# Keeping the last expert block's rows on chip: a one-core trunk layer with a mixture of experts

## The reference, cut to what matters

```python
def trunk_layer(x, ...):                                   # T = 1024 prompt + 64 sample tokens, D = 1024
    z = rms_norm(x, norm1_g) @ w_in                        # 12 chunks of 128 columns: pool, value, gate
    ...pooling mixer, conv mixer...
    x = x + concat([y_pool, y_conv]) @ w_out + b_out
    hm = rms_norm(x, norm2_g)
    x = x + hier_moe(hm, ...)                              # then the final rms_norm with norm_f_g

def hier_moe(h, ...):
    ...group g_sel, top 2 of its 8 experts: eid[token, 2], gates[token, 2]
    order = argsort(flat_e)                                # rows sorted by expert, blocks of 128 rows
    yb = (silu(xb @ w_eg[e]) * (xb @ w_eu[e])) @ w_ed[e]   # per block
    y = zeros.at[buf_tok].add(yb * buf_gate[:, None])      # each token adds its two rows
```

## Time and profile before

| what | us |
|---|---|
| median of 3 runs (991.07 to 991.28) | 991.25 |
| the profiled execution's own time | 992.78 |
| its span, first to last instruction | 990.9 |
| TensorE busy (share of the span) | 945.9 (95%) |
| VectorE busy | 840.9 (85%) |
| ScalarE busy | 586.6 (59%) |
| GpSimd busy | 168.4 (17%) |
| mean granted TensorE clock | 0.988 |

### The profile page before, as it was taken

The page is one execution under the profiler, slowest core; times in us unless marked ns, Lnnn a source line. Parts: engine busy times, 40 slices in busy tenths (PEclk is TensorE's granted clock), DMA queues, the critical chain, the costliest instruction groups (busy, mean ns, idle before and its releaser), DMA issues.

```text
span 990.9 us, 14018 instructions
## 1 busy us (share of the span) xinstructions
PE 945.9 (95%) x4771; PEld 801.5 (81%) x4771; DVE 840.9 (85%) x978; ACT 586.6 (59%) x564; POOL 168.4 (17%) x201
## 2 busy tenths in 40 slices
PE   5999999999999989999999999999999999999973
PEld 5999978987888777788888888888888888888751
DVE  6488998988687697999898998989989899898857
ACT  7311111574532144888777887778877788777514
POOL 1000000000000021632231222312223122231210
PEclk9999999999999979999999999999999999999997
DMA  9321251314332846899999999999999999999988
GB/s 286 118 65 43 67 154 58 112 34 161 128 128 86 329 130 222 335 403 378 401 370 389 378 379 392 384 385 391 387 403 379 397 392 380 397 389 384 340 267 311
DMA packets 68028, 275.72 MB, mean 278 GB/s; under 512 B 12783, under 2 KB 27631, under 8 KB 43417
## 3 DMA queue, kind: packets, MB, share of 16 engines
q1 hardware_dynamic: 56281, 255.97, 68.7%
q0 software_dynamic: 9792, 17.85, 4.7%
q10 hardware_dynamic: 1920, 1.44, 0.6%
HBM read 259.34 MB, written 31.38 MB: 293 GB/s over the span
## 4 chain that ended last, share of the span: by engine, by line
PE 57%; DVE 4%; DMA 2%; ACT 1%; issue 1%; SPq 0%; POOLq 0%; POOL 0%; DVEq 0%; ACTq 0%
PE ps L1234 11%; PE ps L1236 11%; PE ps L1235 11%; PE ps L1253 6%; PE ps L1251 6%; PE ps L1252 6%; PE ps L1206 3%; DVE big L1808 2%; PE ps L1260 1%; DMA y_scratch<-arena,cur 1%; ACT arena L947 1%; DMA arena<-y_scratch 1%; DVE arena L1905 0%; PE ps L1347 0%; PE ps L1190 0%
## 5 line engine op out<-in xcount | busy, mean ns | idle before, releaser
L1808 DVE TENSOR_TENSOR big<-arena,big 128x2048 fp32r<-128x2048 f32 x128 | 286.9, 2283 | 0.0
L843 ACT ACTIVATE big<-arena 128x2048 fp32r<-128x2048 f32 x128 | 238.8, 1910 | 3.5 <-DMA arena<-in_w_eg 1.8
L1234 PE MATMUL ps<-big,ring 128*128 128x512 f32 x508 | 201.1, 396 | 3.2 <-DVE big L1808 3.2
L1236 PE MATMUL ps<-big,ring 128*128 128x512 f32 x508 | 198.0, 390 | 0.0
L1235 PE MATMUL ps<-big,ring 128*128 128x512 f32 x508 | 197.6, 389 | 0.0
L1808 DVE TENSOR_TENSOR slot_tail<-arena,slot_tail 128x2048 fp32r<-128x2048 f32 x62 | 138.9, 2281 | 0.0
L843 ACT ACTIVATE slot_tail<-arena 128x2048 fp32r<-128x2048 f32 x62 | 115.5, 1918 | 0.2 <-DVE eob L1784 0.2
L1234 PEld LDWEIGHTS ps<-big,ring 128*128 128x128 f32 x508 | 95.4, 188 | 22.6 <-DVE big L1808 4.0
L1236 PEld LDWEIGHTS ps<-big,ring 128*128 128x128 f32 x508 | 95.3, 188 | 20.3
L1235 PEld LDWEIGHTS ps<-big,ring 128*128 128x128 f32 x508 | 95.5, 188 | 18.7
L1251 PE MATMUL ps<-slot_tail,hTr 128*128 128x512 f32 x248 | 99.2, 400 | 0.0
(11 more groups left out here) (280 smaller groups left out, 1485.3 us busy)
## 6 DMA issues: line engine op xcount, KB each, us to landing
arena<-in_w_eg SPq DMA_DIRECT2D x64, 1024.0 KB, 8.5
arena<-in_w_eu SPq DMA_DIRECT2D x64, 1024.0 KB, 9.5
arena<-in_w_ed SPq DMA_DIRECT2D x64, 1024.0 KB, 9.9
arena<-in_x_prompt SPq DMA_DIRECT2D x16, 512.0 KB, 5.1
arena<-y_scratch SPq DMA_DIRECT2D x16, 512.0 KB, 8.8
arena<-in_w_in SPq DMA_DIRECT2D x12, 512.0 KB, 4.0
arena<-in_conv_band SPq DMA_DIRECT2D x8, 576.0 KB, 4.3
arena<-in_w_out SPq DMA_DIRECT2D x8, 512.0 KB, 4.1
```

Of the source, the lines that this page charges most:

```text
L843: act.activation(we_h[n % SLOTS], raw[n % RAWS], ACT.Copy).then_inc(high_done, 1)
L1234: pe.matmul(out, part_h[b][:, k, :], wh[:, i, :], start=(k == 0), stop=False)
L1236: ins = pe.matmul(out, part_l[b][:, k, :], wh[:, i, :], start=False, stop=(k == KD - 1))
L1808: dve.tensor_tensor(we_l[n % SLOTS], raw[n % RAWS], we_h[n % SLOTS].bitcast(F32), ALU.subtract).then_inc(low_done, 1)
```

## The change

1. Block 31's rows are no longer scattered. ScalarE copies the product out of PSUM times a per-row gate (`own_h`), VectorE makes the low part (`own_l`, in `keep_low`). A 0/1 matrix per tile (`at_token`), built by VectorE from the slot table, puts row i on its token when TensorE multiplies it by `own_h` and `own_l`. The gate of each row comes by way of DRAM: ScalarE writes the gates (`gate_dram`), POOL gathers one per row (`gate_row`). For this `set_gates` runs before the low parts of the last two pieces.
2. The second rows of all tokens are set to zero early (`zero_second`), because those of block 31 are now never written. SP waits only for the scatter of block 30 before it loads second rows, each tile has its own semaphore and place, and no load waits for a sum.
3. TensorE sums gate times second row and block 31's row for all 9 tiles, and the residual too for tiles 1 and 2; VectorE adds the residual for the other 7 (`add_late`). The 40 idle transposes ahead of the sums are gone.
4. Head: weight chunks are stored so that a chunk is contiguous; (0, 0) is made tile by tile in matmuls of 128, 128 and 108 columns behind tiles 2, 3 and 4, the idle transposes of tiles 2 and 3 are gone, and (1, 0) and (0, 1) follow in pieces.
5. First pair: the two empty scatters move ahead of the wait for `hm_out`; VectorE makes the first rows' low part before `overflow_counts`, pieces 7 and 9 before `hidden` and `overflow_plan`.

```diff
@@ over_loop @@
+        def over_loop(eng, body, ahead=None):      # runs ahead() only if there is an overflow pair
...
@@ sync @@
-                src = w_in[0, :, CHUNKS[j]:CHUNKS[j] + P].rearrange("(k p) n -> p k n", p=P)
-                sp.dma_start(w_raw[j % 3].rearrange("p (k n) -> p k n", k=KD), src).then_inc(w_in_s[j % 3], 16)
+                sp.dma_start(w_raw[j % 3], w_in_chunk[CHUNKS[j] // P, :, :]).then_inc(w_in_s[j % 3], 16)
...
+            def zero_second(t):
+                r = ROWS[t]
+                dst = y2_dram[2 * t * P:2 * (t * P + r), :].rearrange("(p k) n -> p k n", k=2)[:, 1, :]
+                src = MS.rearrange("p t e -> p (t e)")[0:r, 0:D // 4].unsqueeze(1).to_broadcast([r, 4, D // 4])
+                sp.dma_start(dst.rearrange("p (a n) -> p a n", a=4), src).then_inc(zeroed, 16)
+            sp.wait_ge(const_done, 1)
             for j in (4, 5, 6, 7, 8, 9):
                 load_w_in(j)
+                for t in range(j - 4, NT, 6):
+                    zero_second(t)
...
             for b in range(2):
                 sp.wait_ge(gath[b], 16 * n_pairs + 16)
-                sp.wait_ge(scat[b], 16 * n_pairs + 16)
-            for t in range(FB):
+            sp.wait_ge(scat[0], 16 * n_pairs + 16)
+            sp.wait_ge(f_half, 1)
+            for t in range(NT):
+                if t >= FB:                                  # FB was 6, is 4
+                    sp.wait_ge(f_half, t - FB + 1)
                 load_second(t)
...
-                if t + FB < NT:
-                    if t in ON_PE:
-                        sp.wait_ge(f_sum_pe, sums_of(t)[1])
-                    else:
-                        sp.wait_ge(f_acc, sums_of(t)[0])
-                    load_second(t + FB)
@@ scalar @@
+            act.wait_ge(gates_set, 1)
+            act.dma_start(gate_dram.rearrange("(t p) o -> p (t o)", p=P), gates[:, 1, :],
+                          allow_slow_non_contiguous=True).then_inc(gates_out, 16)
             result(PAIRS - 1, 0)
             hidden_high(PAIRS - 1, 1)
-            result(PAIRS - 1, 1, end=True)
-            over_loop(act, over_body)
+            act.wait_ge(piece_used, after(PAIRS, EARLIER[-1], True))
+            act.wait_ge(gate_in, 16)
+            act.activation(own_h, ye_ps, ACT.Copy, scale=gate_row).then_inc(own_high, 1)
...
+            for t in range(NT):
+                if t == 4:
+                    act.wait_ge(f_in[0], 16)
+                act.activation(gate_diag[t], ident[:, :], ACT.Copy, scale=gates[:, 1, t:t + 1]).then_inc(diag_set, 1)
@@ tensor @@
+            BY_TILE = {2: (0, P), 3: (P, 2 * P), 4: (2 * P, IW)}
-            PIECEWISE = {4: ((0, 0, 3),), 5: ((0, 3, 6),), 6: ((0, 6, 8),), 7: ((1, 0, 3),), 8: ((1, 3, 8),)}
+            PIECEWISE = {5: ((1, 0, 0, 3),), 6: ((1, 0, 3, 6),), 7: ((1, 0, 6, 8), (0, 1, 0, 3)), 8: ((0, 1, 3, 8),)}
...
-            quiet_ps = banks(7, 1)
-            for i in range(40):
-                pe.transpose(quiet_ps[:, i % 4 * P:(i % 4 + 1) * P], ident[:, :], ident[:, :])
...
+            pe.wait_ge(own_high, 1)
+            pe.wait_ge(own_low, 1)
+            for t in range(NT):
+                r = ROWS[t]
+                pe.wait_ge(f_half, t + 1)
+                if t in ALL_ON_PE:                           # (1, 2)
+                    for c0 in (0, BANK):
+                        pe.matmul(f_sums[t][0:r, c0:c0 + BANK], ident[0:r, 0:r], x_in[t][0:r, c0:c0 + BANK], start=True, stop=False)
+                elif t - 4 in ALL_ON_PE:
+                    pe.wait_ge(f_y, t - 3)
+                elif t >= 4:
+                    pe.wait_ge(f_acc, added(t - 4))
+                pe.wait_ge(diag_set, t + 1)
+                pe.wait_ge(f_in[t], 16)
+                for c0 in (0, BANK):
+                    out = f_sums[t][0:r, c0:c0 + BANK]
+                    pe.matmul(out, gate_diag[t][0:r, 0:r], y_second[t][0:r, c0:c0 + BANK], start=t not in ALL_ON_PE, stop=False)
+                    pe.matmul(out, at_token[t][:, 0:r], own_h[:, c0:c0 + BANK], start=False, stop=False)
+                    ins = pe.matmul(out, at_token[t][:, 0:r], own_l[:, c0:c0 + BANK], start=False, stop=True)
+                ins.then_inc(f_late, 1)
@@ vector, body(0, first=True) @@
-                    overflow_counts()
                 rows_low(j, 0)
                 if first:
+                    overflow_counts()
                     overflow_blocks()
                     rows_low(j, 1)
...
                 low(j, 6)
-                if not first:
+                if first:
+                    low(j, 7)
+                else:
                     rows_low(j, 1)
                 hidden(j, 0)
-                low(j, 7)
+                if not first:
+                    low(j, 7)
                 low(j, 8)
+                low(j, 9)
                 if first:
                     overflow_plan()
-                low(j, 9)
                 hidden_low(j, 0)
                 low(j, 10)
                 low(j, 11)
@@ vector, end @@
+            dve.memset(gate_row, 0.0)
+            set_gates()
+            dve.engine_nop().then_inc(gates_set, 1)
             ...low parts of LAST, hidden(PAIRS - 1, 1)...
-            set_gates()
+            ...tok_row, tok_in, and two is_equal that write at_token...
+            def keep_low():
+                dve.wait_ge(own_high, 1)
+                dve.scalar_tensor_tensor(own_l, ye_ps, gate_row, own_h.bitcast(F32), ALU.mult, ALU.subtract).then_inc(own_low, 1)
+            def add_late(t):
+                r = ROWS[t]
+                dve.wait_ge(f_half, t + 1)
+                dve.wait_ge(f_late, t + 1)
+                dve.tensor_tensor(x_in[t][0:r, :], f_sums[t][0:r, :], x_in[t][0:r, :], ALU.add).then_inc(f_acc, 1)
+            for t in range(6):
+                add_first(t)
+            keep_low()
+            for t in range(6, NT):
+                add_first(t)
+            dve.wait_ge(gf_in, 16)
             for t in range(NT):
-                add_first(t)
-            for t in range(NT):
-                if t not in ON_PE:
-                    combine(t)
+                if t not in ALL_ON_PE:
+                    add_late(t)
                 ...final(t - 1)...
@@ gpsimd @@
+            pool.wait_ge(gb_in, 32)
+            for b in range(2):
+                scatter(b, s_idx[:, 0:1])
             ...waits for hm_out, x2_out, x2tr_done...
-            for b in range(2):
-                scatter(b, s_idx[:, 0:1])
             pool.wait_ge(idx_done, 1)
             gather(0, g_idx)
...
+            pool.wait_ge(gates_out, 16)
+            pool.indirect_dma_start(out=gate_row, out_offset=None, in_=gate_dram,
+                                    in_offset=bass.IndirectOffsetOnAxis(ap=g_idx[:, E - 1:E], axis=0),
+                                    bounds_check=last_token, oob_is_err=False).then_inc(gate_in, 16)
             pool.sem_inc(cur_done, 1)
             store_rows(PAIRS - 1, 0)
-            pool.sem_inc(cur_done, 1)
-            store_rows(PAIRS - 1, 1)
```

More of the change, by code:

```diff
@@ L200, in trunk_kernel @@
         gf_bc = arena[:, 2 * NT * D:(2 * NT + 1) * D]
[L201 removed]
+        y_second = [arena[:, (2 * NT + 1 + s) * D:(2 * NT + 2 + s) * D] for s in range(FB)] + y_first[0:NT - FB]
+        assert (2 * NT + 1 + FB) * D <= SZ_V + SZ_U + SZ_H + SZ_W + SZ_S1 + SZ_T + SZ_S2 + SZ_X
+        own_h, own_l = big[:, 4 * HP:4 * HP + D], big[:, 4 * HP + D:4 * HP + 2 * D]
+        at_token = [big[:, 8 * HP + t * P:8 * HP + (t + 1) * P] for t in range(KD)] + [hot_mem[:, 0:P]]
+        assert 8 * HP + KD * P <= 2 * KD * T and SLOTS >= 4
         assert RAWS * HP == 12 * D
[L205 removed]
+        ALL_ON_PE = (1, 2)
         ident = sb("ident", [P, P])
@@ L228, in trunk_kernel @@
         act_t = plin.rearrange("p g d -> p (g d)")
-        gate_diag = [plin[:, i, :] for i in range(len(ON_PE))]
+        gate_diag = [plin[:, t, :] for t in range(4)] + [r_g[:, t * P:(t + 1) * P] for t in range(NT - 4)]
         stat = sb("stat", [P, 6, NT])
@@ L284, in trunk_kernel @@
         ye_ps = banks(5, 2)
-        f_sums = {t: banks(2 * i, 2) for i, t in enumerate(ON_PE)}
+        f_sums = [banks(t % 4 * 2, 2) for t in range(NT)]
         const_done = sem("const_done")
@@ L290, in trunk_kernel @@
         xt_in = [sem("xt_in0"), sem("xt_in1")]
-        xa_in = [sem(f"xa_in{t}") for t in range(NT)]
+        tile_in = [sem(f"tile_in{t}") for t in range(NT)]
         wo_in = [sem(f"wo_in{s}") for s in range(4)]
@@ L320, in trunk_kernel @@
             "zero_done"))
-        f_x = [sem(f"f_x{t}") for t in range(NT)]
-        f_in = [sem(f"f_in{s}") for s in range(FB)]
+        f_in = [sem(f"f_in{t}") for t in range(NT)]
         f_half = sem("f_half")
@@ L325, in trunk_kernel, with added @@
         f_out = sem("f_out")
[L326 to L331, removed]
+        diag_set, f_late = sem("diag_set"), sem("f_late")
+        own_high, own_low, gates_set = map(sem, ("own_high", "own_low", "gates_set"))
```

(23 more changed lines are left out.)

104 lines of the change are left out of this document (57 added, 47 removed).

## The result

The changed kernel takes 1004.14 us at the median of four executions (1002.82 to 1006.66), the kernel before 991.26 beside it: a ratio of 1.0125, 95% interval 1.0105 to 1.0145. The forecast was 988.8 (985.0 to 995.5). The profiled execution took 1002.82 (span 1001.0), 10.0 more than the profiled one of before, where the steps had it 2.5 less: a miss of 12.5 us.

What follows compares the result with a forecast made beforehand. TensorE was taken to bound the loop, without slack; head -2.5, first pair -2.7 and end +2.7 sum to -2.5 us, so 991.25 becomes 988.8 us, range 985.0 to 995.5 (own range 986.3 to 991.3).

Steps and rivals of the forecast that it cites:

- Head: Start of the kernel: narrow products at 0.11 us each let (0, 2) start at 37.7, not 40.22: -2.5 us.
- rival (b): Head: narrow products cost two passes, +5.1 us, total 996.4; chance 0.13.
- First pair: First pair of blocks: earlier gather and low parts, two stalls gone: -2.7 us, bounds -3.75 to 0.
- POOL now finds its two empty scatters done ... 0.8 earlier: First pair: with the empty scatters moved ahead, the gather goes out near 360.8, 0.8 us earlier, bounds 0.6 and 1.0.
- What comes late next: First pair: the 4.0 us plan now stands ahead of pieces 10 and 11, leaving 2.7 of the 3.75 us gain.
- Rival (d): First pair gains nothing, its gather and loads landing when they did: total +0.2, 991.5 us; chance 0.10.
- the gates' trip: End: gates' store takes 7.3 us, gather 1.3; block 30 leaves 1.4 us later, under the backlog: no cost.
- Rival (a): End: gates' store takes 14.6 us and delays block 30's scatter; total +2.1, 993.4 us; chance 0.17.
- the start without the trip: End: TensorE's first sum at 956.7, 17.9 us after block 30's copy, when second rows land.
- the load of the first second rows: End: after block 30's scatter lands at 949.7, first second rows land at 956.5, between 954.5 and 960.9.
- the sums: End: 29.3 us from TensorE's start to tile 8's add, VectorE slower from tile 3; 19.5 us before.

Runs made afterwards that it cites:

- run 7: Kernel before with the new head alone (chunked weights, narrow first products): 989.33 us, ratio 0.9977 to the kernel before.
- run 3: Kernel before with the new head and the new order of the first pair, old end kept: 988.86 us, ratio 0.9969.
- run 4: Changed kernel with the gates stored as 128 runs of 36 bytes, not 1152 elements of 4 bytes (block 31's gates wrong): 996.17 us, ratio 1.0037.
- run 2: Changed kernel with gates made and stored during the first pair instead of behind the last: 998.72 us, ratio 1.0071.
- run 5: Changed kernel without the gates' store and gather: VectorE applies each token's gate, own part of tiles 0 to 3 made early: 989.44 us, ratio 0.9978.
- run 6: run 5's kernel with first rows of tiles 6 to 8 loaded behind second rows of tiles 1 to 3: 987.82 us, ratio 0.9956.
- run 9: The kernel of run 6 measured again, unchanged, in five rounds beside the kernel before: 987.36 us, ratio 0.9951.

## Why the prediction was wrong

*Head: right in mechanism, and near in size.* (0, 2) was forecast at 37.7 and starts at 37.32, with 0.11 us a product; rival (b), two passes, falls. By the router 0.5 us more had come, which I had not forecast. Alone the head is worth 2.3 us of the median (run 7).

*First pair: half wrong.* No stall is left before pieces 7 and 9, as forecast. The step "POOL now finds its two empty scatters done ... 0.8 earlier" failed: the gather goes out at the same time with or without them (358.30 in run 7, 358.25 in run 3). In run 7 the second empty scatter ends 0.5 us after the index is written; in run 3 nothing stands ahead, and GpSimd still takes 0.83 us from the end of that write to the gather, where I had counted 0.30. What comes late next was priced at 1.0 and is 1.6 in those two traces. Rival (d), -0 instead of -2.7, was nearer: 0.7 in the traces of runs 7 and 3, 1.2 in the changed kernel's, both within the spread of single profiles.

*End: the step that failed is the gates' trip.* The prediction said "The nearest row is the router's load, 1024 pieces of 144 B, 7.3 us" and "Nothing, at that price". The store of 1152 pieces of 4 bytes took 21.8, and its price went to two waits at once. Rival (a) named this mechanism and its price was too small too: 14.6 us, 993.4. The router's load was the wrong row: when its pieces moved, only SyncE's own queue moved (975 packets under 512 B from 23.6 to 25.0 us), so its 7.3 us hold almost nothing of what pieces cost beside another queue; the gates' pieces moved beside rows that took 94.1%. In the same place 144 packets did land in 7.2 us (run 4), and the trip then held block 30's scatter up by 1.1 us, the gather. What the strided store costs with the queue empty no run shows. The Trainium skill (DMA: Bandwidth & Descriptors, Rules for kernel authors) says that a strided last dimension becomes one descriptor per element; the trace agrees, 1168 packets, and that rule should have outweighed a row of 144-byte pieces.

*End: the start without the trip.* I put it at 17.9 us after block 30's copy, "nearer the fast end because block 31's scatter no longer moves in that stretch". It is 21.2 to 23.2 (runs 2, 4, 5), at the slow end of my bounds or beyond. Block 30's scatter took the 8.8 us that I had priced (8.0 to 8.8 in these runs). The term that was too small is the load of the first second rows: 6.8 us from issue to landing (949.7 to 956.5), and 10.8, 9.3 and 12.0 in the runs. It stands behind the first rows of tiles 6 to 8, and with those out of its way it took 7.2 and 8.4 (runs 6 and 9). Run 4, which keeps the trip, starts 3.6 us later than forecast: 1.1 is the gather, 2.5 this load.

*End: the sums.* 30.5 against 29.3, but by another bound: TensorE, not VectorE (the stretches above; run 5, with less on TensorE, has 23.6). The low clock was there as forecast, 0.50 (1.2 GHz) from 963 to 966 after 19 us of waiting, but the first tile took 5.1 us where I had 4.1. From tile 3 on TensorE takes 2.64 us a tile, where I had VectorE at 2.76; that the whole is so near is in part luck.

Taken together 7.2 us of the miss are pieces, 3.6 the gather and the load of second rows, 1.2 sums, 0.6 the two front parts. With nothing but the 7.2 put into the forecast, its end is +9.9 and its sum +4.7: a loss. And with the pieces gone the change still loses: run 4 is 4.2 us above the kernel before.

## What to carry to other kernels

Price a DMA by its number of pieces and by what fills the engines at that moment, and take the row for it from a stretch with the same load; and ask who waits behind the engine that waits. Before a transfer is taken off the end by adding work, look at what stands ahead of it in the queue: here three loads in another order came out level with the same order and a block kept on chip. Values that an engine already holds by token need no trip by row: move the multiplication to where the factor is.

## What the runs showed that I had not expected

One store of 4.5 KB took 7.2, 21.8, 23.7 and 37.3 us, by its pieces and by the loads beside it. It also held those loads up: they moved at 162 GB/s beside 1168 packets and at 414 beside 144, and in the last case a gather that TensorE needed came 5.19 us late. The scatter of block 31 took 3.3 or 7.8 us by the order of three loads. The first gather of rows, in two profiles of one kernel, let TensorE start its first turn at 368.19 (run 6) or 366.58 (run 9), and block 30's copy came at 937.81 or 933.67; what sets that spread was not settled, and it is larger than the 2.7 us that the first pair was meant to gain.
